# A transformer block on one core: the plan that fills attention and recurrence with projection work is laid out anew, and ScalarE drains part of it

## The reference, cut to what matters

```python
for layer in range(2):                       # d = 1024, 512 latent tokens x, 256 context tokens ctx
    mod_l = silu(c) @ w_mod[layer] + b_mod[layer]       # 6 x 1024 values; mod_c the same from c_ctx
    p_l = split(modulate(rmsnorm(x), mod_l[0], mod_l[1]) @ w_in[layer])       # p_c from ctx
    a = diff_attention(p[0:3])               # "DA": 4 heads, two softmaxes each
    b = hgrn2_mixer(p[3:8])                  # "HG": gated recurrence, both directions
    n = neighbourhood_attention(p[8:11])     # "NA"
    w = window_gqa(p[11:14])                 # "SW"
    x = x + mod_l[2] * (concat(a, b, n, w) @ w_out[layer])
    x = x + mod_l[5] * (relu(modulate(rmsnorm(x), mod_l[3], mod_l[4]) @ w_ff1)**2 @ w_ff2)
    # ctx goes the same way in layer 0 only
```

## Time and profile before

| | us |
|---|---|
| median of three runs | 2528.54 (2526.9 to 2532.72) |
| the profiled execution | 2523.21 |
| its span | 2521.4 |
| busy: PE / DVE / ACT / POOL | 2078.6 / 1159.5 / 766.8 / 610.0 |
| L691, the dense products, of the chain that ended last | 53% |

### The profile page before, as it was taken

One profiled execution on the slowest core, in us unless ns is written; L12 is line 12 of the kernel. 1 busy time (PEld: TensorE's weight loads), 2 busy tenths in 40 slices (PEclk: granted clock), 3 DMA queues, 4 the chain that ended last, 5 costly groups with the idle time before them and its releaser, 6 DMA issues.

```text
span 2521.4 us, 29860 instructions
## 1 busy us (share of the span) xinstructions
PE 2078.6 (82%) x12484; PEld 1705.4 (68%) x12484; DVE 1159.5 (46%) x1782; ACT 766.8 (30%) x1225; POOL 610.0 (24%) x263
## 2 busy tenths in 40 slices
PE   5779786687775698999999997879688639899998
PEld 3667564466664586888888885658477536688887
DVE  2544536555499715222221316454685884522322
ACT  2522222223333325222221315232344432522321
POOL 0121010001166122222222221301001552344432
PEclk9889797778898798999999998989799778999999
DMA  7312020323165011122112212111001011232231
GB/s 261 59 51 84 1 67 1 101 88 80 42 204 193 5 51 49 52 67 67 57 62 67 68 50 39 55 33 34 17 18 51 0 34 51 67 100 88 96 100 67
DMA packets 178918, 168.86 MB, mean 67 GB/s; under 512 B 29200, under 2 KB 176096, under 8 KB 178656
## 3 DMA queue, kind: packets, MB, share of 16 engines
q1 hardware_dynamic: 176704, 161.18, 20.9%
q10 hardware_dynamic: 2080, 5.77, 0.8%
HBM read 159.07 MB, written 2.10 MB: 64 GB/s over the span
## 4 chain that ended last, share of the span: by engine, by line
PE 67%; DVE 17%; ACT 9%; issue 4%; POOL 2%; DMA 1%; ACTq 0%; SPq 0%; DVEq 0%; POOLq 0%
PE gp L691 53%; PE sp L823 3%; PE gp L858 2%; ACT DA_p L1184 2%; POOL HGx_kd L613 2%; PE sp L734 1%; PE tp L838 1%; ACT nt L1097 1%; PE sp L814 1%; PE gp L712 1%; DVE small L1578 1%; DVE sp L1453 1%; PE sp L921 1%; DVE sp L1452 1%; DMA raw<-in_w_mod 1%
## 5 line engine op out<-in xcount | busy, mean ns | idle before, releaser
L637 POOL TENSOR_TENSOR wlo<-raw,whi 128x2048 fp32r<-128x2048 f32 x98 | 452.4, 4617 | 1684.3 <-ACT whi L1079 1684.1
L691 PE MATMUL gp<-xhi,whi 128*128 128x512 f32 (+1 forms) x1584 | 584.1, 369 | 114.5 <-DVE xlo L1473 53.0
L691 PE MATMUL gp<-xlo,whi 128*128 128x512 f32 (+1 forms) x1584 | 570.8, 360 | 0.0
L691 PE MATMUL gp<-xhi,wlo 128*128 128x512 f32 (+1 forms) x1584 | 569.3, 359 | 0.0
L691 PEld LDWEIGHTS gp<-xhi,whi 128*128 128x128 f32 x1584 | 312.1, 197 | 170.2 <-issue 55.8
L691 PEld LDWEIGHTS gp<-xlo,whi 128*128 128x128 f32 x1584 | 311.7, 197 | 43.0 <-issue 1.7
L691 PEld LDWEIGHTS gp<-xhi,wlo 128*128 128x128 f32 x1584 | 310.8, 196 | 43.2
L1079 ACT ACTIVATE whi<-raw 128x2048 fp32r<-128x2048 f32 x98 | 186.8, 1908 | 426.3 <-PE gp L691 425.2
L1833 DVE SCALAR_TENSOR_TENSOR xT<-gp,mods,xT 128x512 f32<-128x512 f32 x120 | 78.6, 662 | 475.9 <-PE gp L691 475.9
L691 PE MATMUL gp<-hhi,whi 128*128 128x512 f32 (+1 forms) x768 | 273.7, 356 | 9.3 <-ACT frel L1393 6.3
L691 PE MATMUL gp<-hlo,whi 128*128 128x512 f32 (+1 forms) x768 | 272.1, 354 | 0.0
(11 more groups left out here) (304 smaller groups left out, 2864.3 us busy)
## 6 DMA issues: line engine op xcount, KB each, us to landing
raw<-in_w_ff SPq DMA_DIRECT2D x64, 1024.0 KB, 5.3
raw<-in_w_mod SPq DMA_DIRECT2D x48, 1024.0 KB, 5.3
raw<-in_w_in SPq DMA_DIRECT2D x20, 1024.0 KB, 5.1
raw<-in_w_in SPq DMA_DIRECT2D x24, 256.0 KB, 4.3
raw<-in_w_out SPq DMA_DIRECT2D x8, 768.0 KB, 4.7
bias<-e SPq DMA_DIRECT2D x96, 32.0 KB
xin<-in_x ACTq DMA_DIRECT2D x1, 2048.0 KB, 9.2
raw<-in_w_out SPq DMA_DIRECT2D x16, 128.0 KB, 4.7
```

The source lines that it names most:

```text
L637: nc.gpsimd.tensor_tensor(wlo[:, s % 2, :, :], raw[:, index[splits[s]] % 2, :, :], whi[:, s % 2, :, :].bitcast(F32), ALU.subtract).then_in ...
L691: mm = pe.matmul(out, lhs, rhs, start=(i == 0 and j == 0), stop=(i == KT - 1 and j == 2))
```

## The change

The plan is laid out anew: every group gets a slot of its own at the middle of its share of the stage, modulation units keep off the slots just before a unit's first group, and they are spread over both layers: NA0 4, SW0 0, DA0 8, HG0 12, then NA1 2, DA1 6, HG1 8. `after_unit` no longer asks that the unit two before v be reached if that is a split unit (its landing is waited for all the same). VectorE reads out all groups of a slot but the last ahead of `finish(n + 1)`. In the recurrence ScalarE, in place of VectorE, reads out modulation groups: slot idx-1 right behind the exponentials of step idx.

```diff
@@ fill_plan
+    counts = {("NA", 0): 4, ("SW", 0): 0, ("DA", 0): 8, ("HG", 0): 12, ("NA", 1): 2, ("SW", 1): 0, ("DA", 1): 6, ("HG", 1): 8}
...
+            for i, item in enumerate(items):
+                slots[(2 * i + 1) * n // (2 * len(items))].append(item)
...
+                a = max((2 * i + 1) * n // (2 * counts[m, l]), free)
+                while opens(a) and a < n - 1:
+                    a += 1
+                slots[a].insert(1 if slots[a] and slots[a][0][1] == "turn" else 0, (u, "row"))
+                slots[a + 1].insert(0, (u, "turn"))
@@ ScalarE, after_unit
-                reached[0] = max(reached[0], index[u])
+                reached[0] = max(reached[0], last_group(u))
...
-                    if index[v] - 2 > reached[0]:
+                    before = units[index[v] - 2]
+                    if before[0] == "mod" and last_group(before) > reached[0]:
                         return
...
-                    if s >= 2 and last_group(splits[s - 2]) > last_group(u):
+                    if s >= 2 and last_group(splits[s - 2]) > reached[0]:
@@ ScalarE, new
+            def modulation(u, c):
+                n = N(u, c)
+                act.wait_ge(group_done, n + 1)
+                if c == "row":
+                    ins = nc.scalar.activation(mrow[:, :], bank(n)[:, 0:UC], ACT.Copy)
+                else:
+                    _, l, j, i = u
+                    for r in range(2):
+                        row = 8 * j + 2 * i + r
+                        ins = nc.scalar.activation(mods[:, l, row, :], bank(n)[:, 2 * r:2 * r + 2], ACT.Identity,
+                                                   bias=pcol[:, l, R_BMOD + row:R_BMOD + row + 1])
+                ins.then_inc(bank_free[group_bank[n]], 1)
...
+                    if own:
+                        modulation(u, c)
@@ ScalarE, recurrence
-                        if idx >= 4:
-                            fill(FILL["HG", l][idx - 4])
+                        if idx >= 1:
+                            fill(FILL["HG", l][idx - 1], own=True)
...
-                for slot in FILL["HG", l][-5:]:
-                    fill(slot)
+                for slot in FILL["HG", l][-2:]:
+                    fill(slot, own=True)
@@ VectorE, attention
+                    fill(FILL[m, l][n][:-1])
                     finish(n + 1)
-                    fill(FILL[m, l][n])
+                    fill(FILL[m, l][n][-1:])
                     output(n)
@@ VectorE, recurrence
-                    if idx >= 1:
-                        fill(FILL["HG", l][idx - 1])
-                fill(FILL["HG", l][-2])
-                fill(FILL["HG", l][-1])
```

More of the change, by code:

```diff
@@ L134, in fill_plan @@
 def fill_plan():
-    mods = [("mod", 0, j, i) for j in range(2, 6) for i in range(4)] + [("mod", 1, j, i) for j in range(6) for i in range(4)]
+    mods = [("mod", l, j, i) for l, js in ((0, range(2, 6)), (1, range(6))) for j in js for i in range(4)]
+    counts = {("NA", 0): 4, ("SW", 0): 0, ("DA", 0): 8, ("HG", 0): 12, ("NA", 1): 2, ("SW", 1): 0, ("DA", 1): 6, ("HG", 1): 8}
     plan = {}
@@ L139, in fill_plan, with opens @@
         tiles = 6 if l < DEPTH - 1 else 4
[L140 to L155, removed]
+        for m, names, n in (("NA", ("SWq", "SWkv"), 2 * tiles), ("SW", ("DAq", "DAk", "DAv"), 2 * tiles),
+                            ("DA", ("HGq", "HGi"), 4 * tiles), ("HG", (), 6 * tiles)):
+            items = [(("prj", l, name), c) for name in names for c in chunks_of(("prj", l, name))]
+            slots = [[] for _ in range(n + 1)]
+            for i, item in enumerate(items):
+                slots[(2 * i + 1) * n // (2 * len(items))].append(item)
+            def opens(a):
+                later = [x for slot in slots[a:] for x in slot if x[0][0] != "mod"]
+                return later and later[0][1] == chunks_of(later[0][0])[0]
+            free = -1
+            for i in range(counts[m, l]):
+                u = mods.pop(0)
+                a = max((2 * i + 1) * n // (2 * counts[m, l]), free)
[3 more added lines that the diff above has]
+                slots[a + 1].insert(0, (u, "turn"))
+                free = a + 1
             plan[m, l] = slots
@@ L1057, in link @@
                 act.wait_ge(act_step, steps[0])
-            nexts, reached = [0], [-1]
+            nexts, reached = [0], [0]
             last_group = lambda u: N(u, "row" if u[0] == "mod" else chunks_of(u)[-1])
             def after_unit(u):
-                reached[0] = max(reached[0], index[u])
+                reached[0] = max(reached[0], last_group(u))
                 while nexts[0] < len(splits):
@@ L1067, in after_unit @@
                     v = splits[s]
-                    if index[v] - 2 > reached[0]:
+                    before = units[index[v] - 2]
+                    if before[0] == "mod" and last_group(before) > reached[0]:
                         return
-                    before = units[index[v] - 2] if index[v] >= 2 else None
-                    if before and before[0] == "mod" and last_group(before) > last_group(u):
-                        return
-                    if s >= 2 and last_group(splits[s - 2]) > last_group(u):
+                    if s >= 2 and last_group(splits[s - 2]) > reached[0]:
                         return
@@ L1079, in after_unit, with fill @@
                     nc.scalar.activation(whi[:, s % 2, :, :], raw[:, index[v] % 2, :, :], ACT.Copy).then_inc(hi_done, 1)
-            def fill(slot):
+            def modulation(u, c):
[10 more added lines that the diff above has]
+                ins.then_inc(bank_free[group_bank[n]], 1)
+            def fill(slot, own=False):
                 for u, c in slot:
+                    if own:
+                        modulation(u, c)
                     if c == ("row" if u[0] == "mod" else chunks_of(u)[-1]):
@@ L1461, in norm @@
                 if which == 1:
-                    wait_read(dve, ("mod", 0, 1, 3) if l == 0 else ("mod", DEPTH - 1, 5, 3))
+                    wait_read(dve, ("mod", l, 1, 3))
                 sh, sc = (0, 1) if which == 1 else (3, 4)
```

## The result

The changed kernel takes 2543.15 us (median of 4 runs, 2539.18 to 2548.43) where the kernel before takes 2530.3 beside it: a ratio of 1.0061, 95% interval 1.0042 to 1.0081. It is slower by 0.6%. I had forecast 2524, with 0.28 on slower. The profiled execution took 2543.85 us, its span is 2542.0, so 20.6 over the span of before, where my sum had 4.6 less. The time lies inside my range, 2504 to 2546, near its upper edge, and on the other side of no change than the forecast.

The account below looks back on a forecast made before the run. The prediction took TensorE to bound SW0, a chain through all engines DA0 and DA1, and VectorE the recurrences; its terms summed to -4.6 us, 2523.2 to 2518.6 for the profiled execution, a median of 2524, range 2504 to 2546.

Parts of the forecast that it names:

- DA1, +19 forecast: Layer 1's differential attention: groups all on odd slots and six modulation units lengthen the stage by 19 us.
- an odd slot is different: DA1: probabilities at 6.3 us, then turning, token group and product with v in sequence, 11.5 us a pair instead of 10.3.
- DA0, -42 forecast: Layer 0's differential attention: waits -37, units -7, clock -11, late maxima +7.5, odd slots +5, in all -42 us.
- With the waits gone I take DA1's clock: DA0: the granted clock rises from 0.76 to DA1's 0.91, worth some 11 us on twelve groups.
- the 7.5 and the 5 of the sum: DA0: late maxima delaying groups behind T or R cost 7.5 us; groups on odd slots cost 5 us.
- The slower rival: Differential attention: the clock stays low, taking back 20 us on DA0's ten groups, 2544 us; chance 0.26.
- The faster rival: Recurrence hides ScalarE's 11 us of late reads and DA1's odd slots cost half (-10), 2503 us; chance 0.24.
- the hole: Recurrence, once a layer: ScalarE's rounding of out 0 waits for its load, exponentials come 8 us late, 6.3 reach VectorE.
- NA0 and SW0, -15 forecast: SW0 -13 us from two waits and two units gone; NA0 -2 us from four turns read out earlier.
- the rival of late rounding: SW0: early rounding fails, DAk's `wlo` stays late and 6.4 us of wait remain, 2530 us; chance 0.06.
- -4.7 + 6 = +1.3: HG0: VectorE freed of reads gains at most 4.7 us; ScalarE's late reads of 12 units cost 6.
- NA1, +11 forecast: Layer 1's NA1: two more units +3.4, waits behind them +3, late SWkv rounding delaying v's copies +4.3 us.

Follow-up runs that it names:

- a_da1none: a_hgdve with DA1's six modulation units moved to HG1, projection groups staying on odd slots: 2517.0 us, ratio 0.9954.
- a_hgdve: The changed kernel with VectorE again reading the recurrence's modulation groups and ScalarE's roundings in their old place: 2529.4 us, ratio 1.0003.
- a_even: The changed kernel with the differential attention's projection groups on even slots: 2527.2 us, ratio 1.0.
- b_drain: The kernel before with VectorE's new order alone, turned groups read ahead of the row sums: 2482.2 us, ratio 0.9814.
- b_hg34: b_both with DA0's 12 modulation units moved to HG0, 34 units there: 2482.4 us, ratio 0.9803.
- b_both: The kernel before with VectorE's new order and the earlier rounding condition, plan and recurrence read-outs as before: 2481.3 us, ratio 0.981.
- a_tail: The changed kernel with ScalarE's roundings released by the recurrence's slots done only behind its last read-out: 2530.5 us, ratio 1.0006.
- b_act_tail: b_both with ScalarE reading the recurrence's 22 units and rounding the output projection only behind the read-outs: 2483.8 us, ratio 0.9823.

## Why the prediction was wrong

**DA1, +19 forecast, +36.1 measured: the step that failed.** I wrote "an odd slot is different" and summed a pair as 6.3 + 0.6 + 3.1 + 1.5 = 11.5 out of rows at full clock. a_da1none shows the chain is right and its durations are not: 13.8, because the placement that puts group and product on one slot leaves the other empty, TensorE stands for the exponentials there, and the next turning and group run at the lower level. In the changed kernel itself the first seven pairs took 16.6, 18.4, 12.8, 18.3, 17.2, 14.1 and 14.7 us, where the sum had 14.0, 16.0, 11.5, 15.2, 13.8, 11.5 and 13.5: each is 1.2 to 3.4 us longer than its term. Of the +19, 12 were for the units and 7 for the placement. Placement alone, without a unit in the stage, costs 26.5 us (123.3 against 96.8), and the six units on top 10.3 (133.6 in a_hgdve against 123.3), 1.7 each: the units were priced rightly and the placement was not. Taken in the other order the placement is worth 19.2 (a_even) and the units 16.9, so the two do not simply add, but the placement is over its 7 us either way.

**DA0, -42 forecast, -29.5 measured: the same mistake.** "With the waits gone I take DA1's clock" was worth 11 us in the sum: the clock is 0.78, and these 11 are nearly the whole miss of 12.5. The waits behind turns went as predicted (37.2 to 3.2), and b_drain shows that the new order does it alone (-31.9). Waits for exponentials and probabilities grew by 12.5 us, as much as the 7.5 and the 5 of the sum together. b_drain with 12 units at a clock of 0.85 takes 153.9 us, the changed kernel with 8 at 0.78 takes 156.3: four units fewer, 7 us by b_hg34's price, gave nothing. With the four groups of DA0's odd slots on even ones the stage was 2.8 us shorter (a_even), no more than its spread; what else it is was not isolated.

Both steps come to 12.5 + 17.1 = 29.6 us, more than the 25 by which the sum missed. The slower rival named this mechanism, and its 2544 is nearly the measured time, but that is luck: it put 20 us on DA0's groups alone, where the two stages were 29.6 over, and NA0 with SW0 gave 11.8 more than forecast. It should have had DA1's groups too, and more than its 0.26. The faster rival was half right: once the hole is gone the late reads show in no kernel's time, but odd slots cost more and not half.

**NA0 and SW0, -15 forecast, -26.8 measured.** In NA0 the 6.0 us of waits behind turns are 1.9, and the clock is 0.98 instead of 0.93. In SW0 the two waits of the earlier trace rows are gone, as forecast (the rival of late rounding is out), but two units fewer give, together with the new places of the groups, 7.0 us (after against b_both), 3.5 each and not 1.7.

**The recurrences, +20.9 forecast, +25.8 with what follows them.** The hole was right in place and cause and nearly in size: I had 6.3 us a layer in the steps, and the last step is 7.4 longer than in a_tail in both. Its second half, at the last read-out, I had at 1: the read-outs grew by 4.3 and 5.0. The rest of the recurrences I had at -4.7 + 6 = +1.3 and at +5, and without the hole they are 3.4 and 4.8 us longer than before (a_tail). That is luck in the sizes, since ScalarE's late reads are not the cause: with VectorE reading (a_hgdve) they are 3.1 and 6.7 longer. What makes them longer is not isolated. VectorE with 22 units less to read did not get faster (b_act_tail: steps of 154.1 us and not 150.4). The Trainium skill (SBUF — State Buffer, Who interferes with whom) says that a VectorE instruction with at most one SBUF input, outside its 2-port modes, does not contend with GpSimd, by which these 4.7 us would not come. The runs agree with that; none isolates the lock itself.

**NA1, +11 forecast, +10.6 measured**, with the late copies of v (ScalarE's 18.35 - 13.95 = 4.4 us, where I had 4.3): right.

**Signs.** The wait for `wlo` went, no wait behind a turn in DA0 is over 1.3 us, and the hole and the late copies came as named. DA0 near 143 us and DA1 near 119 did not come; DA0 over 155 us was my own mark for wrong.

## What to carry to other kernels

Where TensorE takes part in a chain through other engines, price its work at the clock of the schedule you are making, not of the rows you read: ask where TensorE will stand after the move, and put the fill there. A wait on a load must not stand in the queue of an engine that others need every 2.7 us; move the bookkeeping that triggers it, here behind the last read-out. Read out early what holds a bank, before long work whose result is needed later, and try such an order alone before changing the plan around it.

## What the runs showed of the hardware

Six unread products a step raised the granted clock in DA1 from 0.76 to 0.89 and shortened the stage by 5.8 us. None of the 22 waits of TensorE in DA1 in the changed kernel is longer than 4.5 us, most are 0.6 to 1.8, and the clock still falls from 2.4 to 1.2 GHz again and again (token groups of the earlier trace rows at 1.00, of the changed kernel at 0.50). The Trainium skill (TensorE: Matmul & The Clock Gate, A second HAM failure mode: psum-queue depth-cycling) tells of another kernel whose clock swings between the two levels because TensorE idles briefly but often between groups of products. This trace agrees.

A stage with more work in it was the shorter one: HG0 took 152.7 us with 12 modulation units at a clock of 0.87, 150.4 with 22 at 0.95, and 148.5 with 24 at 0.96, VectorE reading in all three. The placement differs too, so the clock's share is not shown by these three alone. The limit was the loads: 24 were hidden, 34 were not.
